# Cached latent attention: four sequences at once on the column quarters, all pages resident

## The chip, the cores and the metric

The kernel runs on one core of one Trainium2 chip. The metric is device time in microseconds (us). Every array is float32; matmuls of plain float32 operands appear in the trace as two records each, transposes as one.

## The reference

One decoder layer is computed for a prompt of 1024 positions and for 8 sample sequences of 4 new tokens each. Two token mixers run side by side: dilated window attention and multi-head latent attention. The change concerns the latent attention of the sample sequences, over 1024 cached positions that lie in pages of 128:

```python
ckv_past = cache_ckv[i][page_table].reshape(n_dec, past_len, B_KV_LORA)     # (8, 1024, 256)
kpe_past = cache_kpe[i][page_table].reshape(n_dec, past_len, B_ROPE_DIM)    # (8, 1024, 32)

def mla_sample(q_nope, q_pe, ckv_ext, kpe_ext, w_uk, w_uv):
    scale = (B_NOPE_DIM + B_ROPE_DIM) ** -0.5
    q_lat = jnp.einsum('nthe,che->nthc', q_nope, w_uk)
    s = (einsum('nthc,nkc->nhtk', q_lat, ckv_ext)
         + einsum('nthr,nkr->nhtk', q_pe, kpe_ext)) * scale
    p, _ = masked_softmax(s, jnp.arange(l)[None, :] <= qpos[:, None])
    o_lat = einsum('nhtk,nkc->nthc', p, ckv_ext)
    return einsum('nthc,che->nthe', o_lat, w_uv)
```

Each sequence has 8 heads x 4 tokens = 32 query rows, scored against 1028 keys (1024 cached, 4 new). A key has a latent part of 256 numbers, which serves as the value too, and a rotary part of 32.

## The kernel before

The program is a series of blocks with barriers between them: projections, the prompt's latent attention (`attend_latent`), the sample's latent attention (`attend_sample` with kind "latent"), the prompt's window attention, the sample's window attention (`attend_sample` with kind "window"), and a long tail (merge, output projection, MLP, embedding). Within a block each engine has its own list of instructions, in an order written out by hand, with semaphores between them.

`attend_sample` for the latent kind treats one sequence after another. A page number is read from an on-chip table into a register (line 1390) and the page is loaded (line 1391): the latent part by SyncE (SP), 128 KB a page, the rotary part by GpSimd (POOL). Keys live in a ring of four buffers `ls_keys`; the first is filled while `attend_latent` still runs (class `Ahead`, lines 1341 to 1375). For each of 8 tiles of 128 keys `turn_tile` transposes two latent halves (line 1522) and the rotary part (line 1524) into bank 3 or 4; ScalarE copies the even tiles and VectorE the odd ones to SBUF (lines 1445 to 1454, `take_keys`). `scores` multiplies the 32 query rows with the turned keys (1542 latent, 1544 rotary), into partitions 0 to 31. VectorE adds the mask and finds the maximum (1658), ScalarE takes the exponent (1461), VectorE divides (1665), TensorE transposes the probabilities (1553, 1554), VectorE copies them (1671, 1672). `values` multiplies them with the pages as loaded (1566) and with the new rows (1568); the result is copied (1709), transposed (1576) and copied again (1687). TensorE interleaves one tile's transposes for the sequence after next with one tile's value matmuls. After all sequences a projection with `w_uv` (1611) and four VectorE operations (1717, 1719) end the stage. In the middle of the stage SP also loads three of the four 1 MB pieces (`win_nat`) with which the next stage starts (1311).

`attend_latent` fills SP's list with the first pages and with eight copies of the cached window values from HBM to HBM (line 607), each waiting for a step of TensorE. Its scores and values (993, 1015) and the window stage's (1168, 1174, 1203, 1210) already use parts of the array: 1015 writes two column halves in turn, 1168 four column quarters with two row halves.

Lines that matter:

```python
            def scores(s):                      # 1525 on
                        for k in range(2):
                            pe.matmul(out, g.ql_t[:, k, s].rearrange("p h t -> p (h t)"), key_t[:, k, at:at + w],
                                      start=k == 0, stop=False)
```

Of the kernel before, what the change touches and what calls it, by code (L numbers as in the profile page):

```python
# [27 lines left out]
F32 = mybir.dt.float32  # L28
F32R = mybir.dt.float32r
I32 = mybir.dt.int32  # L30
ALU = mybir.AluOpType
# [3 lines left out]
P = 128  # L35
# [10 lines left out]
H = 8  # L46
# [10 lines left out]
SK = 5  # L57
EPS = 1e-6
# [85 lines left out]
def build(nc, io):  # L144

    with ExitStack() as ctx:
# [43 lines left out]
        g.w_uv_sb = room("w_uv_sb", [P, 2, H * E])  # L190
        g.ckv_t = room("ckv_t", [P, 2, T])
# [16 lines left out]
        g.latent_mask = Room(nc, Ahead.start_of("latent") - SEQ * BYTES)("latent_mask", [P, NT - 1, P])  # L208
# [737 lines left out]
def attend_latent(g, ahead):  # L946
# [151 lines left out]
RES = 4  # L1098
# [242 lines left out]
class Ahead:  # L1341
# [3 lines left out]
    @staticmethod  # L1345
    def start_of(kind):

        size = 2 * SK * H * E if kind == "window" else NPAGE * (KL + RD) + NSEQ * NPAGE
        return TOP // 32 * 32 - size * BYTES

    def __init__(self, g, kind):
        self.kind, self.start = kind, self.start_of(kind)
        room = Room(g.nc, self.start)
        if kind == "window":
            self.keys, self.vals = (room(f"ws_{n}0", [P, SK, H * E]) for n in ("keys", "vals"))
            self.k_in, self.v_in = ([g.sem(f"ws_{n}_in{j}") for j in range(3)] for n in "kv")
        else:
            self.keys = self.vals = room("ls_keys0", [P, NPAGE, KL + RD])
            self.pages = room("ls_pages", [1, NSEQ * NPAGE], I32)
            self.k_in, self.v_in = ([g.sem(f"ls_{n}_in{j}") for j in range(4)] for n in ("ckv", "kpe"))  # L1360
            self.pages_in = g.sem("pages_in")

    def load(self, g, sp):

        if self.kind == "window":
            load_cached_window(sp, g.cache_win_k, 0, self.keys, self.k_in[0])
            load_cached_window(sp, g.cache_win_v, 0, self.vals, self.v_in[0])
        else:
            sp.dma_start(self.pages[:, :], g.page_table.rearrange("(a s) n -> a (s n)", a=1)).then_inc(self.pages_in, 16)
            sp.wait_ge(self.pages_in, 16)  # L1370
            load_pages(sp, self.pages, 0, g.cache_ckv, self.keys[:, :, :KL], self.k_in[0])
# [15 lines left out]
def load_pages(eng, pages, s, cache, dst, arrived):  # L1387

    for n in range(NPAGE):
        page = eng.value_load(pages[0:1, s * NPAGE + n:s * NPAGE + n + 1], min_val=0, max_val=NPHYS - 1)  # L1390
        eng.dma_start(dst[:, n, :], cache[0, bass.ds(page, 1)].rearrange("a p c -> p (a c)")).then_inc(arrived, 16)  # L1391


def attend_sample(g, kind, ahead):
# [6 lines left out]
    window = kind == "window"  # L1401
    tag = "ws" if window else "ls"
    tiles = SK if window else NPAGE
    width = tiles * P + TDEC
    vcols = H * E if window else KL
    room = Room(nc, R2, RW if window else g.room_kept)
    sem = lambda name: g.sem(f"{tag}_{name}")
    if window:
        keys = [ahead.keys] + [room("ws_keys1", [P, SK, H * E])]
        vals = [ahead.vals] + [room(f"ws_vals{j}", [P, SK, H * E]) for j in (1, 2)]  # L1410
        unit_room(g, Room(nc, RW, RX), "tail")
        key_t = room("ws_key_t", [P, H // 2, width])
        q_new = room("ws_q_new", [NS, H * E])
        k_new = room("ws_k_new", [NS, H * E])
        k_new_t = room("ws_k_new_t", [P, H // 2, NS])
        q_rows = room("ws_q_rows", [P, H // 2, NSEQ, H, TDEC])
        v_new = room("ws_v_new", [TDEC, 3, H * E])
        v_new_in = [sem(f"v_new_in{j}") for j in range(3)]
    else:
        keys = [ahead.keys] + [room(f"ls_keys{j}", [P, NPAGE, KL + RD]) for j in (1, 2, 3)]  # L1420
        vals = keys
        key_t = room("ls_key_t", [P, 2, width])
        pe_t = room("ls_pe_t", [RD, width])
        v_new = room("ls_v_new", [TDEC, NSEQ, KL])
        o_t = room("ls_o_t", [P, 2, H, NSEQ, TDEC])
    mask = room(f"{tag}_mask", [NS, width])
    masked = room(f"{tag}_masked", [NS, width])
    prob = room(f"{tag}_prob", [NS, width])
    prob_t = room(f"{tag}_prob_t", [P, tiles + 1, NS])
# [13 lines left out]
    def take_keys(eng, s, odd):  # L1443
# [4 lines left out]
        for n in range(odd, tiles, 2):  # L1448
# [4 lines left out]
            if not window:  # L1453
                last = copy(pe_t[:, cols], g.bank[:RD, 3 + odd, 2 * P:3 * P])
# [746 lines left out]
```

## Time and profile before

| | us |
|---|---|
| median of 3 runs (2176.5 to 2183.6) | 2182.46 |
| the profiled execution | 2187.04 |
| its span | 2185.3 |

| engine | busy in the span | in the sample's latent stage (137.8 us) |
|---|---|---|
| TensorE matmul | 2077.8 us, 95% | 128.2 us |
| VectorE | 825.4 us, 38% | 47.1 us |
| ScalarE | 473.6 us, 22% | 26.2 us |
| GpSimd | 723.1 us, 33% | 30.7 us |

The span runs from the first to the last instruction; the execution's own time lies 1.7 us above it. The stage of the change runs from 714.6 to 852.4 us. The granted TensorE clock is given as a share of full speed: 1.00 is 2.4 GHz, 0.50 is 1.2 GHz.

### The profile page before, as it was taken

Reading aid. Unit: us, or ns where it says so; the run is one execution under the profiler, and the core shown is the slowest. Engines: PE = TensorE matmul, PEld = TensorE weight load, DVE = VectorE, ACT = ScalarE, POOL = GpSimd, SP = SyncE. Lnnn points to the kernel's source line nnn. Section 1 sums busy time; section 2 is a strip of 40 time slices with the busy share of each in tenths; the row PEclk is TensorE's granted clock in tenths of the full one; section 3 lists DMA queues with packets and bytes.
Section 4 is the critical chain, followed back from the end, with each engine's and each line's share of the span. In section 5 each row is a group of like instructions: output and inputs, shape, how many; then the busy total and the mean of one; then the engine's idle time right before and its main releaser. Section 6 shows DMA issues by size and latency. Waiting matters only on the chain. (4 is left out here: it accounts for less than half of the span.)

```text
span 2185.3 us, 34746 instructions
## 1 busy us (share of the span) xinstructions
PE 2077.8 (95%) x13121; PEld 1765.5 (81%) x13121; DVE 825.4 (38%) x1889; ACT 473.6 (22%) x1036; POOL 723.1 (33%) x483
## 2 busy tenths in 40 slices
PE   7899999999999898889989999999999999999898
PEld 7877799963566334663379999999999999999897
DVE  4245011153566334673334543212211211245565
ACT  4231111121455222551101211001100100112222
POOL 4223033300000320001036656535634644566431
PEclk9999999999999899999999999999999999999999
DMA  6333464400223443216354111111111111111212
GB/s 210 89 114 121 156 238 166 154 11 10 99 78 116 126 126 97 60 44 202 118 191 134 49 39 39 49 48 49 41 48 48 48 49 46 41 49 48 69 30 80
DMA packets 179831, 192.72 MB, mean 88 GB/s; under 512 B 11398, under 2 KB 152582, under 8 KB 178950
## 3 DMA queue, kind: packets, MB, share of 16 engines
q1 hardware_dynamic: 162854, 162.01, 23.4%
q10 hardware_dynamic: 14816, 28.12, 3.7%
q0 software_dynamic: 2048, 1.05, 0.2%
q8 instruction: 75, 1.23, 0.2%
q14 instruction: 38, 0.31, 0.0%
HBM read 160.74 MB, written 63.97 MB: 103 GB/s over the span
## 5 line engine op out<-in xcount | busy, mean ns | idle before, releaser
L635 PE MATMUL bank<-h_hi,wu_hi_tail 128*128 128x352 f32 x960 | 311.4, 324 | 3.4 <-POOL wu_lo_tail L1960 3.4
L636 PE MATMUL bank<-h_lo,wu_hi_tail 128*128 128x352 f32 x960 | 308.8, 322 | 0.0
L637 PE MATMUL bank<-h_hi,wu_lo_tail 128*128 128x352 f32 x960 | 308.7, 322 | 0.0
L1958 POOL TENSOR_TENSOR wu_hi_tail<-w_stage_tail,ones 128x1024 fp32r<-128x1024 f32 x88 | 169.9, 1931 | 407.1 <-DMA w_stage_tail<-in_w_ob 185.6
L635 PE MATMUL bank<-a_hi,wu_hi_tail 128*128 128x352 f32 x768 | 247.7, 323 | 0.0
L636 PE MATMUL bank<-a_lo,wu_hi_tail 128*128 128x352 f32 x768 | 246.1, 320 | 0.0
L637 PE MATMUL bank<-a_hi,wu_lo_tail 128*128 128x352 f32 x768 | 245.9, 320 | 0.0
L1960 POOL TENSOR_TENSOR wu_lo_tail<-w_stage_tail,wu_hi_tail 128x1024 fp32r<-128x1024 f32 x88 | 219.7, 2496 | 6.9
L635 PEld LDWEIGHTS bank<-h_hi,wu_hi_tail 128*128 128x128 f32 x960 | 180.9, 188 | 3.7 <-issue 3.7
L636 PEld LDWEIGHTS bank<-h_lo,wu_hi_tail 128*128 128x128 f32 x960 | 181.2, 189 | 0.0
L637 PEld LDWEIGHTS bank<-h_hi,wu_lo_tail 128*128 128x128 f32 x960 | 181.0, 189 | 0.0
L1915 ACT ACTIVATE a_hi<-f_hg 128x352 f32 x96 | 48.0, 500 | 602.8 <-DVE f_hg L2021 602.8
L2004 DVE TENSOR_TENSOR x_res<-bank,x_res 128x352 f32 x120 | 62.9, 525 | 300.6 <-PE bank L637 300.4
L1391 POOL DMA_DIRECT2D ls_keys<-in_cache_kpe x64 | 35.6, 556 | 349.1 <-issue 349.1
L636 PEld LDWEIGHTS bank<-a_lo,wu_hi_tail 128*128 128x128 f32 x768 | 144.3, 188 | 0.0
L635 PEld LDWEIGHTS bank<-a_hi,wu_hi_tail 128*128 128x128 f32 x768 | 144.1, 188 | 0.0
L637 PEld LDWEIGHTS bank<-a_hi,wu_lo_tail 128*128 128x128 f32 x768 | 143.9, 187 | 0.0
L1970 POOL TENSOR_TENSOR a_lo<-f_hg,a_hi 128x352 f32 (+1 forms) x96 | 91.2, 950 | 144.9 <-ACT a_hi L1915 144.9
L2018 DVE TENSOR_TENSOR f_tmp<-bank,rstd_bc 128x352 f32<-128x352 f32 x96 | 50.3, 524 | 234.6 <-PE bank L637 234.4
L432 PE MATMUL bank<-wn_hi,h_hi 128*128 128x512 f32 (+5 forms) x360 | 133.7, 371 | 0.0
L434 PE MATMUL bank<-wn_hi,h_lo 128*128 128x512 f32 (+5 forms) x360 | 131.7, 366 | 0.0
L433 PE MATMUL bank<-wn_lo,h_hi 128*128 128x512 f32 (+5 forms) x360 | 131.2, 364 | 0.0
(288 smaller groups left out, 3968.5 us busy)
## 6 DMA issues: line engine op xcount, KB each, us to landing
w_stage_tail<-in_w_up SPq DMA_DIRECT2D x32, 512.0 KB, 4.0
w_stage_tail<-in_w_down SPq DMA_DIRECT2D x32, 512.0 KB, 3.6
gate_d<-gate_out ACTq DMA_DIRECT2D x16, 528.0 KB, 2.9
f_gates<-gate_d ACTq DMA_DIRECT2D x24, 352.0 KB, 3.1
w_stage_gates<-in_w_in SPq DMA_DIRECT2D x16, 512.0 KB, 3.8
ls_keys<-in_cache_ckv SPq DMA_DIRECT2D x64, 128.0 KB, 2.1
ws_keys<-in_cache_win_k SPq DMA_DIRECT2D x8, 1024.0 KB, 7.2
ws_vals<-in_cache_win_v SPq DMA_DIRECT2D x8, 1024.0 KB, 6.5
```

Of the source, the lines that this page charges most:

```text
L432: pe.matmul(out, a, w, start=k == 0, stop=False)
L433: pe.matmul(out, a, v, start=False, stop=False)
L434: last = pe.matmul(out, c, w, start=False, stop=k == KD - 1)
L635: pe.matmul(out, w, a, start=n == 0, stop=False)
L636: pe.matmul(out, w, b, start=False, stop=False)
L637: last = pe.matmul(out, v, a, start=False, stop=n == len(ks) - 1)
L1915: act.activation(chunk_of(st.out[0], i, q), g.hg[:, q % 2:q % 2 + 1, :], ACT.Copy).then_inc(g.hi_s, 1)
L1958: pool.tensor_tensor(g.wu_hi[:, j], g.w_stage[:, j], one, ALU.mult).then_inc(g.w_hi, 1)
L1960: pool.tensor_tensor(g.wu_lo[:, j], g.w_stage[:, j], g.wu_hi[:, j].bitcast(F32), ALU.subtract).then_inc(g.w_split, 1)
L1970: pool.tensor_tensor(chunk_of(st.out[1], i, q), g.hg[:, q % 2:q % 2 + 1, :], chunk_of(st.out[0], i, q).bitcast(F32), ALU.subtract).then_in ...
L2004: dve.tensor_tensor(x, g.bank[:, q:q + 1, :CH], x, ALU.add).then_inc(g.free, 1)
L2018: dve.tensor_tensor(g.tmp[:, q % 2, :], g.bank[:, q, :CH], g.rstd_bc[:, c * CH:(c + 1) * CH], ALU.mult).then_inc(g.free, 1)
```

## The change

The class `Ahead` is split into `CachedPages` and `CachedWindow`, and `attend_sample` into `attend_latent_sample` and `attend_window_sample`; the window part is the same as before. In the latent part:

- Each sequence's pages have a buffer of their own. Three sequences are loaded while `attend_latent` runs (`early = 3`), into places free at that time; the other five at the stage's start, into the places of the prompt's queries, keys and values. Their 40 page numbers are read into registers ahead (`find_rest`), during `attend_latent`.
- All rotary pages are loaded by GpSimd during `attend_latent`, as 32 lines of 4 rows x 32 numbers each instead of 128 lines of 32, four pages one under another.
- Sequences are treated in two batches of four. Sequence s of a batch writes its 32 rows of scores and values to partitions 32s to 32s+31. Mask, exponent and transposes then work on 128 partitions, once per batch.
- Transposes go in groups: two tiles x two halves in one bank and one copy of 512 columns; the rotary keys of a sequence are two transposes. The rotary scores take four matmuls of 128 columns, one for each residue j of the key's position, against queries padded with zeros (`q_pad`), written to every fourth column.
- The new keys are scored by matmuls of their own (4 columns) rather than copied beside the turned keys. The division by the sum moves from the probabilities to the result (32 x 1028 per sequence before, 128 x 256 per batch after).
- SP's order at the stage's start is: 40 pages, four loads of `q_pad`, four of the mask, the new rows, then the three `win_nat` loads for the next stage.

```diff
-        for kind in ("latent", "window"):
-            ahead = Ahead(g, kind)
-            (attend_window if kind == "window" else attend_latent)(g, ahead)
-            attend_sample(g, kind, ahead)
+        pages = CachedPages(g)
+        attend_latent(g, pages)
+        attend_latent_sample(g, pages)
+        cached = CachedWindow(g)
+        attend_window(g, cached)
+        attend_window_sample(g, cached)
...
             for s in range(NSEQ):
                 sp.wait_ge(o_got, s * (N // NSEQ) + 1)
                 copy_cache(sp, g, g.cache_win_v, g.win_v_sample, s, 1)
+                if s == NSEQ // 2:
+                    ahead.find_rest(sp)
...
+class CachedPages:
+    start = TOP // 32 * 32 - (NPAGE * KL + NSEQ * NPAGE) * BYTES
+    early = 3
+    def __init__(self, g):
+        nc = g.nc
+        room = Room(nc, self.start)
+        first_keys = room("ls_keys0", [P, NPAGE, KL])
+        self.pages = room("ls_pages", [1, NSEQ * NPAGE], I32)
+        low = Room(nc, R1 + KD * T * BYTES, R1 + (KD + H // 2) * T * BYTES)
+        kept = Room(nc, R2, g.room_kept)
+        self.key_t = kept("ls_key_t", [P, BATCH, 2, PAST])
+        self.rope_t = kept("ls_rope_t", [P, BATCH, 2, P])
+        self.keys = [first_keys] + [low(f"ls_keys{s}", [P, NPAGE, KL]) for s in range(1, self.early)]
+        self.keys += [kept(f"ls_keys{s}", [P, NPAGE, KL]) for s in range(self.early, NSEQ)]
+        self.v_new = kept("ls_v_new", [TDEC, BATCH, KL])
+        self.rope = []
+        for b in range(2):
+            at = g.ckv_t_at + b * T * BYTES
+            self.rope.append(Room(nc, at, at + SEQ * BYTES)(f"ls_rope{b}", [P, BATCH, 2, RES * RD]))
+        self.pages_in, self.rope_in = g.sem("pages_in"), g.sem("rope_in")
+        self.k_in = [g.sem(f"ls_k_in{s}") for s in range(NSEQ)]
+    def page(self, eng, s, n):
+        at = s * NPAGE + n
+        return eng.value_load(self.pages[0:1, at:at + 1], min_val=0, max_val=NPHYS - 1)
+    def load_keys(self, g, sp, s, page_of):
+        for n in range(NPAGE):
+            src = g.cache_ckv[0, bass.ds(page_of(n), 1)].rearrange("a p c -> p (a c)")
+            sp.dma_start(self.keys[s][:, n, :], src).then_inc(self.k_in[s], 16)
+    def load(self, g, sp):
+        sp.dma_start(self.pages[:, :], g.page_table.rearrange("(a s) n -> a (s n)", a=1)).then_inc(self.pages_in, 16)
+        sp.wait_ge(self.pages_in, 16)
+        for s in range(self.early):
+            self.load_keys(g, sp, s, lambda n: self.page(sp, s, n))
+    def find_rest(self, sp):
+        self.found = {(s, n): self.page(sp, s, n) for s in range(self.early, NSEQ) for n in range(NPAGE)}
+    def load_rest(self, g, sp):
+        for s in range(self.early, NSEQ):
+            self.load_keys(g, sp, s, lambda n: self.found[s, n])
     def load_rotary(self, g, pool):
         pool.wait_ge(self.pages_in, 16)
-        load_pages(pool, self.pages, 0, g.cache_kpe, self.keys[:, :, KL:], self.v_in[0])
+        for s in range(NSEQ):
+            for n in range(NPAGE):
+                lo = RD * (n % 4)
+                src = g.cache_kpe[0, bass.ds(self.page(pool, s, n), 1)].rearrange("a (k j) r -> (a k) (j r)", j=RES)
+                pool.dma_start(self.rope[s // BATCH][lo:lo + RD, s % BATCH, n // 4, :], src).then_inc(self.rope_in, 16)
...
+def attend_latent_sample(g, ahead):
...
+    def take_keys(copy, eng, s, odd):
+        if s >= BATCH:
+            eng.wait_ge(s_full, s // BATCH)
+        for q in range(groups):
+            n = s * groups + q
+            if n % 2 != odd:
+                continue
+            eng.wait_ge(k_full, n + 1)
+            src = g.bank[:, 3 + odd, :]
+            if q < groups - 1:
+                copy(key_t[:, s % BATCH, :, 2 * q * P:2 * (q + 1) * P], src.rearrange("p (k c) -> p k c", k=2)).then_inc(k_got[odd], 1)
+            else:
+                copy(rope_t[:, s % BATCH, :, :].rearrange("p a c -> p (a c)"), src[:, :2 * P]).then_inc(k_got[odd], 1)
+    with nc.Block() as block:
+        @block.sync
+        def _(sp):
+            ahead.load_rest(g, sp)
+            sp.wait_ge(pad_set, 1)
+            for j in range(RES):
+                sp.dma_start(q_pad[RD * j:RD * (j + 1), j, :, :], g.qpe_t[:, :, :, :].rearrange("r s h t -> r s (h t)")).then_inc(pad_in, 16)
+            for j in range(BATCH):
+                sp.dma_start(mask[rows(j), :], g.mask_ls_c).then_inc(mask_in, 16)
+            v_src = g.ckv_sample[0].rearrange("s t c -> t s c")
+            sp.dma_start(v_new[:, :, :], v_src[:, :BATCH, :]).then_inc(v_new_in, 16)
+            load_queries_and_keys(g, sp, (0, 1, 2))
+            sp.wait_ge(o_full, 1)
+            sp.dma_start(v_new[:, :, :], v_src[:, BATCH:, :]).then_inc(v_new_in, 16)
+        @block.gpsimd
+        def _(pool):
+            pool.memset(q_pad[:, :, :, :].rearrange("p j s c -> p (j s c)"), 0.0).then_inc(pad_set, 1)
+        @block.tensor
+        def _(pe):
+            def turn_keys(s):
+                for q in range(groups):
+                    n = s * groups + q
+                    if q == 0:
+                        pe.wait_ge(ahead.k_in[s], 16 * NPAGE)
+                    if n == groups - 1:
+                        pe.wait_ge(ahead.rope_in, 16 * NSEQ * NPAGE)
+                    if n >= 2:
+                        pe.wait_ge(k_got[n % 2], n // 2)
+                    if q < groups - 1:
+                        for k in range(2):
+                            for a in range(2):
+                                at = (2 * k + a) * P
+                                last = pe.transpose(g.bank[:, 3 + n % 2, at:at + P], keys[s][:, 2 * q + a, k * P:(k + 1) * P], g.ident[:, :])
+                    else:
+                        for a in range(2):
+                            last = pe.transpose(g.bank[:, 3 + n % 2, a * P:(a + 1) * P], rope[s // BATCH][:, s % BATCH, a, :], g.ident[:, :])
+                    last.then_inc(k_full, 1)
+            def scores(b):
+                done = groups * BATCH * (b + 1) // 2
+                for odd in range(2):
+                    pe.wait_ge(k_got[odd], done)
+                if b == 0:
+                    pe.wait_ge(pad_in, 16 * RES)
+                else:
+                    pe.wait_ge(s_got, b)
+                    pe.wait_ge(pt_high, b)
+                latent = lambda k, s: g.ql_t[:, k, s].rearrange("p h t -> p (h t)")
+                for c in range(2):
+                    for k in range(2):
+                        for s in batch(b):
+                            pe.matmul(g.bank[rows(s), c, :], latent(k, s), key_t[:, s % BATCH, k, c * 512:(c + 1) * 512],
+                                      start=k == 0, stop=False)
+                    for j in range(RES):
+                        for s in batch(b):
+                            out = g.bank[rows(s), c, :].rearrange("p (n m j) -> p n m j", n=4, j=RES)[:, :, :, j]
+                            pe.matmul(out, q_pad[:, j, s, :], rope_t[:, s % BATCH, c, :].rearrange("p (n m) -> p n m", n=4),
+                                      start=False, stop=j == RES - 1)
+                for k in range(2):
+                    for s in batch(b):
+                        new = slice(SEQ + s * TDEC, SEQ + (s + 1) * TDEC)
+                        pe.matmul(g.bank[rows(s), 2, :TDEC], latent(k, s), g.ckv_t[:, k, new], start=k == 0, stop=False)
+                for s in batch(b):
+                    last = pe.matmul(g.bank[rows(s), 2, :TDEC], g.qpe_t[:, s].rearrange("p h t -> p (h t)"),
+                                     g.kpe_t[:, s * TDEC:(s + 1) * TDEC], start=False, stop=True)
+                last.then_inc(s_full, 1)
+            def turn_probs(b):
+                pe.wait_ge(e_done, b + 1)
+                if b >= 1:
+                    pe.wait_ge(pt_low, b)
+                    pe.wait_ge(pt_high, b)
+                for n in range(NPAGE):
+                    last = pe.transpose(g.bank[:, 5 + n // 4, n % 4 * P:(n % 4 + 1) * P], prob[:, n * P:(n + 1) * P], g.ident[:, :])
+                    if n == 3:
+                        last.then_inc(pt_full, 1)
+                pe.transpose(g.bank[:TDEC, 2, P:2 * P], prob[:, PAST:], g.ident[:, :]).then_inc(pt_full, 1)
+            def values(b):
+                pe.wait_ge(pt_low, b + 1)
+                pe.wait_ge(pt_high, b + 1)
+                pe.wait_ge(v_new_in, 16 * (b + 1))
+                if b >= 1:
+                    pe.wait_ge(ot_got, b)
+                for n in range(NPAGE):
+                    for s in batch(b):
+                        pe.matmul(g.bank[rows(s), 7, :KL], prob_t[:, n, rows(s)], keys[s][:, n, :], start=n == 0, stop=False)
+                for s in batch(b):
+                    last = pe.matmul(g.bank[rows(s), 7, :KL], prob_t[:TDEC, NPAGE, rows(s)], v_new[:, s % BATCH, :], start=False, stop=True)
+                last.then_inc(o_full, 1)
+            def turn_result(b):
+                pe.wait_ge(o_taken, b + 1)
+                for k in range(2):
+                    last = pe.transpose(g.bank[:, 7, KL + k * P:KL + (k + 1) * P], o_nat[:, k * P:(k + 1) * P], g.ident[:, :])
+                last.then_inc(ot_full, 1)
+            for s in batch(0):
+                turn_keys(s)
+            scores(0)
+            turn_keys(4)
+            turn_keys(5)
+            turn_probs(0)
+            turn_keys(6)
+            values(0)
+            turn_keys(7)
+            turn_result(0)
+            scores(1)
+            turn_probs(1)
+            values(1)
+            turn_result(1)
+            pe.wait_ge(ot_got, 2)
...
+        @block.scalar
+        def _(act):
+            copy = lambda out, src: act.activation(out, src, ACT.Copy)
+            def exponent(b):
+                act.wait_ge(s_got, b + 1)
+                act.activation(prob[:, :], prob[:, :], ACT.Exp, scale=-1.0, bias=top[:, b, 0:1],
+                               accum_out=top[:, b, 2:3]).then_inc(e_done, 1)
...
+        @block.vector
+        def _(dve):
+            def largest(b):
+                dve.wait_ge(s_full, b + 1)
+                if b >= 1:
+                    dve.wait_ge(pt_full, 2 * b)
+                dve.tensor_tensor_reduce(out=prob[:, :], in0=g.bank[:, 0:3, :].rearrange("p a b -> p (a b)")[:, :PAST + TDEC],
+                                         in1=mask[:, :], scale=-1.0, scalar=-FLOOR, op0=ALU.add, op1=ALU.min,
+                                         accum_out=top[:, b, 0:1]).then_inc(s_got, 1)
...
+            for s in batch(0):
+                take_keys(dve.tensor_copy, dve, s, 1)
+            dve.wait_ge(mask_in, 16 * BATCH)
+            largest(0)
+            take_keys(dve.tensor_copy, dve, 4, 1)
+            take_keys(dve.tensor_copy, dve, 5, 1)
+            invert(0)
+            take_probs(0)
+            take_keys(dve.tensor_copy, dve, 6, 1)
+            take_values(0)
+            take_keys(dve.tensor_copy, dve, 7, 1)
+            take_result(0)
+            largest(1)
+            invert(1)
+            take_probs(1)
+            take_values(1)
+            take_result(1)
...
```

## Rows read from the trace of the kernel before

**Rows 1.** TensorE's timeline at the stage's start: start us, us, line, count [idle before].
```profile
712.31 0.97 PE L1015 MATMUL bank<-latent_prob_t,vb 128*64 128x128 f32 x12
714.64 0.41 PE L1522 MATMUL bank<-ident,ls_keys 128*128 128x128 f32 x2 [1.35 <-PEq L970]
```

**Rows 2.** Stretches: length, busy us of each engine, PEclk, DMA share, GB/s.
```profile
714.64:852.40 137.76, 128.22 (x600) 47.41 (x600) 47.10 (x149) 26.24 (x80) 30.73 (x56) 0.95 0.31 93
745.00:762.00 17.00, 16.83 (x82) 6.23 (x81) 5.87 (x19) 3.27 (x10) 3.11 (x6) 1.00 0.13 38
728.00:731.00 3.00, 1.38 (x10) 0.95 (x11) 1.04 (x4) 1.81 (x6) 1.27 (x3) 1.00 0.49 142
732.00:745.00 13.00, 11.45 (x26) 2.81 (x25) 2.25 (x8) 0.53 (x2) 5.53 (x10) 0.51 0.45 125
```

**Rows 3.** TensorE's timeline: scores at half and full clock, values in a row.
```profile
735.86 3.62 PE L1542 MATMUL bank<-ls_key_t,ql_t 128*32 128x512 f32 x4
...
755.64 1.90 PE L1542 MATMUL bank<-ls_key_t,ql_t 128*32 128x512 f32 x4
...
761.62 0.44 PE L1522 MATMUL bank<-ident,ls_keys 128*128 128x128 f32 x2
...
838.96 3.64 PE L1566 MATMUL bank<-ls_keys,ls_prob_t 128*32 128x256 f32 x16
```

**Rows 4.** Groups by shape, 712 to 853 us: count, busy us, mean ns.
```profile
L1566 PE MATMUL bank<-ls_keys,ls_prob_t 128*32 128x256 f32 x128 | 35.9, 387 | 0.4 <-DVE ls_prob_t L1672 0.4
L1542 PE MATMUL bank<-ls_key_t,ql_t 128*32 128x512 f32 x64 | 33.9, 656 | 0.9 <-DVE ls_pe_t L1637 0.9
L1522 PE MATMUL bank<-ident,ls_keys 128*128 128x128 f32 x128 | 27.5, 302 | 4.6 <-ACT ls_pe_t L1445 2.4 <-PEq L970 1.4 <-DMA ls_keys<-in_cache_ckv 0.6
L1524 PE MATMUL bank<-ident,ls_keys 128*32 128x128 f32 x64 | 17.9, 279 | 0.0
L1544 PE MATMUL bank<-ls_pe_t,qpe_t 32*32 32x512 f32 x32 | 17.5, 628 | 0.0
```

**Rows 5.** TensorE's timeline in the window stage: eight parts of the array, then the next group.
```profile
867.45 0.56 PE L1168 MATMUL bank<-kw_c,qw_c 64*32 64x192 f32 x16 [0.88 <-DVE kw_c L1338]
867.94 0.60 PE L1174 MATMUL bank<-kw_c,qw_c 64*128 64x128 f32 x6
```

**Rows 6.** SP: timeline of the page loads, median of the pieces, sizes and landing.
```profile
578.06 133.40 SPq L607 DMA_DIRECT2D out_win_v_sample<-in_cache_win_v  x8
716.18 13.24 SPq L1391 DMA_DIRECT2D ls_keys<-in_cache_ckv  x12
L1391 SPq DMA_DIRECT2D ls_keys<-in_cache_ckv x64: 332/333/881, 558.1 to 809.5; - x64
1038.33 1.70 SPq L1383 DMA_DIRECT2D ws_keys<-in_cache_win_k  x4
ls_keys<-in_cache_ckv SPq DMA_DIRECT2D x64, 128.0 KB, 2.1
```

**Rows 7.** Timeline of the window's sample stage: groups of four transposes through two banks.
```profile
988.41 1.09 PE L1522 MATMUL bank<-ident,ws_keys 128*128 128x128 f32 x8 [1.44 <-ACT ws_key_t L1445]
989.10 0.60 ACT L1445 ACTIVATE ws_key_t<-bank 128x512 f32<-128x512 f32 x1 [0.74 <-PE bank L1522]
989.53 0.69 DVE L1452 COPY ws_key_t<-bank 128x512 f32<-128x512 f32 x1 [1.77 <-PE bank L1522]
989.75 0.66 PE L1522 MATMUL bank<-ident,ws_keys 128*128 128x128 f32 x4 [0.25 <-ACT ws_key_t L1445]
```

**Rows 8.** A stretch in which 1 MB loads fill the DMA engines (columns as in rows 2).
```profile
764.00:770.00 6.00, 6.00 (x30) 2.37 (x29) 2.43 (x8) 2.29 (x7) 0.45 (x1) 1.00 0.89 278
```

**Rows 9.** Groups of the other engines, and the projection's timeline.
```profile
L1658 DVE CUSTOM_DVE_ANT_0 ls_masked<-bank,ls_mask 32x1028 f32<-32x1028 f32 x8 | 9.7, 1217 | 48.9 <-PE bank L1544 48.9
L1461 ACT ACTIVATE ls_prob<-ls_masked,ls_top 32x1028 f32<-32x1028 f32 x8 | 9.1, 1141 | 17.5 <-DVE ls_top L1658 17.5
849.70 1.15 PE L1611 MATMUL bank<-ls_o_t,w_uv_sb 128*64 128x32 f32 x32 [0.32 <-DVE ls_o_t L1687]
```

More of the change, by code:

```diff
@@ L1384, in load_cached_window @@
     sp.dma_start(dst[:, 1:, :], cache[0, s, PAST // 2:].rearrange("(a p) h e -> p a (h e)", p=P)).then_inc(arrived, 16)
[L1387 to L1394, printed above, removed]
-    nc = g.nc
-    window = kind == "window"
-    tag = "ws" if window else "ls"
-    tiles = SK if window else NPAGE
-    width = tiles * P + TDEC
[L1405 to L1429, printed above, removed]
-    top = room(f"{tag}_top", [NS, 2, 4])
-    o_nat = room(f"{tag}_o_nat", [NS, vcols])
@@ new lines, in attend_window_sample @@
+def attend_window_sample(g, ahead):
+    nc = g.nc
+    tiles = SK
+    width = tiles * P + TDEC
+    vcols = H * E
+    room = Room(nc, R2, RW)
+    sem = lambda name: g.sem(f"ws_{name}")
+    keys = [ahead.keys] + [room("ws_keys1", [P, SK, H * E])]
+    vals = [ahead.vals] + [room(f"ws_vals{j}", [P, SK, H * E]) for j in (1, 2)]
+    unit_room(g, Room(nc, RW, RX), "tail")
+    key_t = room("ws_key_t", [P, H // 2, width])
+    q_new = room("ws_q_new", [NS, H * E])
+    k_new = room("ws_k_new", [NS, H * E])
+    k_new_t = room("ws_k_new_t", [P, H // 2, NS])
+    q_rows = room("ws_q_rows", [P, H // 2, NSEQ, H, TDEC])
+    v_new = room("ws_v_new", [TDEC, 3, H * E])
+    v_new_in = [sem(f"v_new_in{j}") for j in range(3)]
+    mask = room("ws_mask", [NS, width])
+    masked = room("ws_masked", [NS, width])
+    prob = room("ws_prob", [NS, width])
+    prob_t = room("ws_prob_t", [P, tiles + 1, NS])
+    top = room("ws_top", [NS, 2, 4])
+    o_nat = room("ws_o_nat", [NS, vcols])
@@ L1450, in take_keys @@
             cols = slice(n * P, (n + 1) * P)
[L1451 to L1455 removed]
+            copy(key_t[:, :, cols], g.bank[:, 3 + odd, :].rearrange("p (k c) -> p k c", k=4)).then_inc(k_got[odd], 1)
     def exponent(act, s):
@@ L1495, in _ @@
         @block.gpsimd
         def _(pool):
[L1497 to L1507 removed]
+            for j in range(2):
+                pool.wait_ge(g.w_loaded[j], (g.turns + 2) * 16)
+                split_weights(pool, g, j, g.units + j + 1)
@@ L1520, in turn_tile @@
                 b = 3 + n % 2
-                for k in range(4 if window else 2):
+                for k in range(4):
                     last = pe.transpose(g.bank[:, b, k * P:(k + 1) * P], keys[s % k_ring][:, n, k * P:(k + 1) * P], g.ident[:, :])
-                if not window:
-                    last = pe.transpose(g.bank[:RD, b, 2 * P:3 * P], keys[s % k_ring][:, n, KL:], g.ident[:, :])
                 last.then_inc(k_full, 1)
@@ L1567, in values @@
                 else:
-                    pe.matmul(g.bank[:NS, 6, :vcols], prob_t[:TDEC, tiles, :], v_new[:, s % v_ring if window else s, :],
+                    pe.matmul(g.bank[:NS, 6, :vcols], prob_t[:TDEC, tiles, :], v_new[:, s % v_ring, :],
                               start=False, stop=True).then_inc(o_full, 1)
@@ L1604, in _ @@
             turn_result(NSEQ - 1)
-            if not window:
-                pe.wait_ge(ot_got, NSEQ)
-                for h in range(H):
-                    lo = E * (h % 2)
-                    for c in range(2):
-                        last = pe.matmul(g.bank[lo:lo + E, 5 + h % 2, (h // 2) * NS:(h // 2 + 1) * NS], g.w_uv_sb[:, c, h * E:(h + 1) * E],
-                                         o_t[:, c, h].rearrange("p s t -> p (s t)"), start=c == 0, stop=c == 1)
-                last.then_inc(ot_full, 1)
         @block.scalar
```

250 lines of the change are left out of this document (125 added, 125 removed).

## The prediction

> **What bounds the kernel now.** I read the page's shares first, then the busy times of single stretches, then the shapes and the timeline inside the stage that the change rewrites. TensorE is busy in nearly all of the span, in every stage, so a stage is worth what its TensorE work and its waits take, and stages follow each other behind barriers: what one saves, the end saves. The rewritten stage, latent attention over the cached pages, runs from the first transpose of cached keys at 714.64 to the first instruction of the window stage at 852.4: 137.8 us [rows 1, 2]. In it TensorE is busy 128.2 us, and is fully busy in the middle (16.83 of 17 us), while VectorE has 47 us, ScalarE 26 us and the DMA engines 31% [rows 2]. So it is bound by TensorE's own stream, not by data. One sequence costs 15.5 us at full clock (scores 755.64 to 761.62). 13 us of the stage ran at half clock [rows 2, 3].
>
> **What goes.** The old matmuls use 32 of 128 columns: 32 query rows per sequence, always in the first column quarter. By shape they are 64 latent score records of 512 columns, 33.9 us; 32 rotary ones, 17.5 us; 128 value records, 35.9 us; and 192 transposes, 45.4 us [rows 4].
>
> **Do quarters run at once?** The trace of before has no four-quarter matmul over all 128 rows, so I bound it. Four 512-column records in one quarter take 1.90 us with the last one's latency of 0.6, 0.43 to 0.46 apart [rows 3]. Sixteen records of 192 columns on 64 rows by 32 columns (two row halves, four column quarters) start at 867.45 and the next group starts at 867.94: 0.49 us. One after another, at that rate (about 0.16 us for 192), they would take 2.6 us. Twelve records of 128 columns over all 128 rows, alternating between the two column halves, take 0.97 us with the last one's latency of some 0.27, about 0.06 us each, where eight 128-column transposes take 1.09 us, 0.11 each [rows 1, 5, 7]. Halves over 128 rows share fully, quarters over 64 rows share nearly fully. I take four at once; the other end is none at once.
>
> The Trainium skill, "TensorE: Matmul & The Clock Gate", Part 3, gives 2.38 times for three column tiles with 512 columns, some 80% of perfect. By that figure, as an estimate, the streams below would be about 5 us longer. The trace's 0.49 us against 2.6 us already contains such losses.
>
> **What the new stage costs on TensorE, at full clock.**
> - Scores of one batch of four: 32 records of 512 columns are 8 rounds of four, 8 x 0.43 = 3.4 us. 64 rotary records of 128 columns (four residues against a zero-padded query, written with a stride) are 16 x 0.11 = 1.8 us. 24 records of four columns are 0.3 us. With latency 5.6 us, where four sequences took 4 x 6.0 [rows 3].
> - Values of one batch: 72 records of 256 columns, 18 rounds. The old 16 in a row took 3.64 us, 0.217 each [rows 3], so 18 x 0.217 + 0.2 = 4.1 us.
> - Turning keys: per sequence 18 transposes instead of 24 (rotary keys come four rows to a 128-wide line), but in five groups of up to four that go through two banks. The window's sample stage has this very loop: groups start at 988.41 and 989.75 on one bank, the ScalarE copy takes 0.60 and the VectorE copy 0.69, the latter ending at 990.22 [rows 7]. So a pair of groups needs 1.44 us, a group 0.72, a sequence 3.6. Copies bound it, not the transposes.
>
> The strided write of the rotary scores has no row. Nearest are contiguous writes of the same size; below, it costs nothing; above, a rate halved adds 1.8 us per batch. I take nothing.
>
> **When data is there.** Three sequences' pages come during the prompt's latent stage. SP there issues 24 page DMAs instead of 8, at 1.10 us each with its read 18 us more, and reads 40 page numbers between two cache copies, at most 27 us; the queue only waits there to issue 8 copies over 133 us [rows 6]. The last copy waits for its step, at 711, as before. GpSimd issues 64 rotary DMAs there, and was idle. Both cost nothing; if that cover were gone, the loads at the stage's start would come up to 45 us later.
>
> At the stage's start SP issues the other 40 pages. A page took 1.10 us, of which the DMA instruction is 0.33; the rest is reading its number and preparing the address. Without the read a bare load has 0.43 (four in 1.70), and half of the 1.10 would be 0.55 [rows 6]. I take 0.5, address steps included: 20 us. 5.2 MB at the 278 GB/s seen with win_nat loads is 19 us, the same [rows 8]. Behind these, in SP's order, stand the four small DMAs that fill the padded queries and four for the mask, and TensorE's first scores wait for the queries. So scores can start at 714.4 + 20 + 1.7 + 2.1 (landing) = 738.5; the ends are 735 and 741. Four sequences are turned by 714.6 + 14.4 = 729, or 3 later if the fourth's pages hold it. **The new wait is some 9 us of idle TensorE for the padded queries**, and everything after stands behind it.
>
> **From there, at full clock:** scores 5.6; VectorE's mask and maximum 1.3 and ScalarE's exponent 1.35, both ahead of their key copies (1.22 and 1.14 on 32 partitions, taken as the same on 128) [rows 9]; two sequences turned 7.2; probabilities turned 1.1; third sequence 3.6 with 0.9 of probability copies; values 4.1; fourth sequence 3.6; result and last key copy 1.2: 30.0 us. Second batch: 5.6 + 2.65 + 1.1 + 0.9 + 4.1 + 1.1 for the result, 1.15 for the value projection, 1.2 for its four copies and 0.5 to the next stage: 18.3 us [rows 9]. The next stage then starts at 738.5 + 48.3 = 786.8 instead of 852.4: 65.6 us saved.
>
> **The clock.** In before, a stretch where TensorE transposed through two banks and waited (1.38 of 3 us busy at 728 to 731) was followed by 13 us at half clock, from 731 to 745, through 9 us of continuous score matmuls; scores then took 3.62 us where they take 1.90 [rows 2, 3]. The new stage has this kind of stretch for longer, then the idle wait. If everything after 738 ran at half clock, scores add 11.2, values 8.2, transposes and the rest 3, and each of 20 groups 0.2: 26.6 us. I take a third, 9 us: the first scores and part of what follows.
>
> The Trainium skill, same page, Part 4, says transposes do not count as busy for the clock. By that rule the turning stretches would keep the clock low all through; that gives the second case below. The trace is mixed: full clock in the old middle with transposes between value matmuls.
>
> **Sum.** 65.6 - 9 = 56.6 us. The profiled execution took 2187.04 us around a span of 2185.3 and goes to 2130.4; it lies 4.6 above the median of the runs, 2182.46, which goes to **2126 us**.
>
> **Rivals.**
> - Half clock throughout: 2182.5 - 65.6 + 26.6 = 2143.5 us. For it: [rows 2]. Against: dense value and score blocks between.
> - Everything kinder: queries there at 735 and no clock loss: 2182.5 - 69 = 2113.5 us.
> - Quarters take turns, so that the change doesn't do what it says: scores become 32 x 0.43 + 64 x 0.11 + 1.2 = 22 us, values 15.6, which adds 16.4 and 11.5 per batch, 56 us: no change, 2182 us. Against: the 0.49 us of [rows 5].
> - The other side: each change of quarter drains the array, so that every record pays its latency instead of its pitch: 32 x 0.66 + 64 x 0.28 = 39 us of scores (the transposes' 0.28 for 128 columns) and 72 x 0.39 = 28 us of values [rows 4], 57 us more per batch than forecast, 115 us in all: 2126 + 115 = 2241 us. It decides from 28 us more per batch. Against it: the alternating halves of line 1015 [rows 1], 12 records in 0.97 us, where each alone would pay 0.28.
>
> **Chances.** Forecast 0.70, half clock 0.12, kinder 0.12, turns 0.04, drain 0.02. The 80% range is 2109 to 2149: the kinder case less 4 for cheaper issues, and the half-clock case plus 5 for slower pages and the strided writes. Faster by over 0.3% (6.5 us, about what a measurement here can tell): 0.95; same 0.03; slower 0.02.
>
> **What would show it.** Scores of four sequences in about 5.6 us, records of four quarters starting within some 10 ns of each other; values in about 4; TensorE idle before the first scores until the padded queries land, near 738; groups of transposes 0.72 us apart; the window stage starting near 796 with the 9 us of clock loss. It is wrong if the 512-column records of the quarters start 0.4 us apart, if key pages arrive later than 0.5 us each, or if the prompt's latent stage (before 714) gets longer through the added DMAs.

## The result and the profile after

| | before | after |
|---|---|---|
| median of the runs shown | 2181.5 us (4 runs) | 2123.9 us (4 runs, 2122.4 to 2125.6) |
| ratio, with 95% interval | | 0.9727 [0.9707, 0.9746] |
| span of the profiled execution | 2185.3 us | 2121.4 us |

The forecast was 2126 us; 57.6 us were saved where 56.6 were foreseen. Between the two profiled executions the difference is 63.9 us (2187.04 and 2123.12): the one before lies 4.6 us above the median of its runs, the one after 0.8 us below. The timelines give the lengths of the stages from the first instruction of each (the last two borders from SP's first load); "half" is the time that the records show at half clock:

| us | before | half | after | half |
|---|---|---|---|---|
| up to the sample's latent stage | 714.6 | | 713.9 | |
| sample's latent stage | 137.8 | 13.7 | 77.3 | 23.9 |
| window stage | 120.1 | 17.1 | 117.6 | 17.9 |
| window's sample stage | 129.9 | 17.1 | 128.8 | 19.6 |
| tail | 1082.9 | 24.0 | 1083.9 | 25.7 |

So 60.5 of the span's 63.9 us are from the rewritten stage. TensorE's timeline in it, after (answers to [rows 1, 3, 7]):

```profile
713.85 1.06 PE L1511 MATMUL bank<-ident,ls_keys 128*128 128x128 f32 x8 [1.21 <-PEq L975]
...
724.17 1.10 PE L1511 MATMUL bank<-ident,ls_keys 128*128 128x128 f32 x8 [0.57 <-DMA ls_keys<-in_cache_ckv]
725.62 1.09 PE L1511 MATMUL bank<-ident,ls_keys 128*128 128x128 f32 x8 [0.35 <-DVE ls_key_t L1471]
...
739.98 3.64 PE L1530 MATMUL bank<-ls_key_t,ql_t 128*32 128x512 f32 x16 [12.48 <-DMA ls_q_pad<-qpe_t]
743.36 1.40 PE L1535 MATMUL bank<-ls_rope_t,ls_q_pad 128*32 128x128 f32 x32
744.57 1.91 PE L1530 MATMUL bank<-ls_key_t,ql_t 128*32 128x512 f32 x16
746.28 1.06 PE L1535 MATMUL bank<-ls_rope_t,ls_q_pad 128*32 128x128 f32 x32
...
750.84 1.97 PE L1511 MATMUL bank<-ident,ls_keys 128*128 128x128 f32 x8 [2.21 <-ACT ls_key_t L1600]
...
761.20 3.66 PE L1565 MATMUL bank<-ls_keys,ls_prob_t 128*32 128x256 f32 x64
...
769.31 1.92 PE L1530 MATMUL bank<-ls_key_t,ql_t 128*32 128x512 f32 x16 [0.34 <-issue]
...
774.72 0.24 PE L1542 MATMUL bank<-kpe_t,qpe_t 32*32 32x4 f32 x8
777.60 1.49 PE L1552 MATMUL bank<-ident,ls_prob 128*128 128x128 f32 x8 [2.64 <-ACT ls_prob L1604]
...
780.32 5.94 PE L1565 MATMUL bank<-ls_keys,ls_prob_t 128*32 128x256 f32 x64 [1.02 <-issue]
...
791.12 2.37 PE L1328 MATMUL bank<-ident,win_nat 128*128 128x128 f32 x20 [1.58 <-PEq L1475]
```

Sixteen 512-column records, four per quarter, take 1.91 us, where in [rows 3] four in one quarter took 1.90. The second batch's scores run from 769.31 to 774.96, 5.7 us. The idle time of 12.48 us before the first scores ends with the padded queries. SP's timeline in the prompt's latent stage and at the stage's start (answers to [rows 6]):

```profile
557.49 26.40 SPq L1397 DMA_DIRECT2D ls_keys<-in_cache_ckv  x24
583.94 126.88 SPq L612 DMA_DIRECT2D out_win_v_sample<-in_cache_win_v  x8
713.95 22.06 SPq L1397 DMA_DIRECT2D ls_keys<-in_cache_ckv  x40
736.06 2.48 SPq L1482 DMA_DIRECT2D ls_q_pad<-qpe_t  x4
```

Forty pages in 22.06 us are 0.55 us each, and the small loads stand behind all of them. The stage as a whole and pieces of it (columns as in [rows 2]):

```profile
714.60:791.00 76.40, 49.95 (x577) 31.75 (x575) 20.02 (x38) 14.57 (x26) 0.16 (x1) 0.84 0.41 133
728.00:740.00 12.00, 0.03 (x4) 0.06 (x5) 0.00 (x0) 0.00 (x0) 0.00 (x0) 0.60 0.71 212
...
757.00:765.40 8.40, 7.94 (x102) 5.13 (x102) 2.76 (x6) 2.35 (x5) 0.00 (x0) 1.00 0.01 2
...
780.00:787.00 7.00, 6.50 (x72) 3.17 (x72) 0.33 (x3) 0.00 (x0) 0.00 (x0) 0.64 0.01 2
```

TensorE is busy 50 of 76 us where it was 128 of 138. By shape, 714 to 795 us (answers to [rows 4]):

```profile
L1511 PE MATMUL bank<-ident,ls_keys 128*128 128x128 f32 x128 | 19.0, 292 | 6.8 <-ACT ls_key_t L1600 2.8 <-DVE ls_key_t L1471 2.1 <-PEq L975 1.2
L1565 PE MATMUL bank<-ls_keys,ls_prob_t 128*32 128x256 f32 x128 | 9.6, 465 | 1.0 <-issue 1.0
L1530 PE MATMUL bank<-ls_key_t,ql_t 128*32 128x512 f32 x64 | 9.4, 710 | 12.8 <-DMA ls_q_pad<-qpe_t 12.5 <-issue 0.3
L1535 PE MATMUL bank<-ls_rope_t,ls_q_pad 128*32 128x128 f32 x128 | 4.6, 285 | 0.0
```

The same 128 value records take 9.6 us instead of 35.9, the same 64 latent score records 9.4 instead of 33.9.

### The profile page after: what moved, and what is told of

It is laid out like the page before. It is cut to its first block, busy times and chain, and to the rows that moved or that the text cites. A ratio compares the mean times of both kernels' runs of the same rounds, so it can differ in the third digit from the quotient of the medians.

```text
span 2121.4 us, 34495 instructions
## 1 busy us (share of the span) xinstructions
PE 2001.8 (94%) x13103; PEld 1752.9 (83%) x13103; DVE 796.7 (38%) x1778; ACT 460.9 (22%) x982; POOL 721.2 (34%) x484
## 4 chain that ended last, share of the span: by engine, by line
PE 46%; DVE 1%; DMA 1%; issue 1%; POOL 1%; ACT 1%; DVEq 0%; ACTq 0%; POOLq 0%
PE bank L640 15%; PE bank L641 15%; PE bank L642 15%; DMA f_gates<-gate_d 1%; DVE x_res L2254 0%; PE bank L2321 0%; PE bank L2282 0%; DVE f_diag L2339 0%; PE bank L2284 0%; PE bank L2283 0%; PE bank L2358 0%; DMA out_y_prompt<-y_nat 0%; PE bank L2311 0%; POOL wu_lo_tail L2177 0%; DVE f_hg L2252 0%
## 5 line engine op out<-in xcount | busy, mean ns | idle before, releaser
L640 PE MATMUL bank<-h_hi,wu_hi_gates 128*128 128x352 f32 x384 | 124.7, 325 | 3.7 <-PEq L311 3.7
```

Source lines behind the costliest of these rows:

```text
L640: pe.matmul(out, w, a, start=n == 0, stop=False)
```

## The experiments

All are edits of the changed kernel. Ratios are to the kernel before, runs on the same chip; "stage" is the sample's latent stage in the profiled execution (77.3 us in the changed kernel). The experiments ran in three series on three chips, where the kernel before had medians of 2183.6, 2182.2 and 2183.8 us against 2181.5 beside the changed kernel. So a difference of medians between rows can be some 2 us off; the ratios are free of this, and where the two differ the text gives both.

| run | median us | ratio, 95% interval | stage us |
|---|---|---|---|
| changed kernel | 2123.9 | 0.9727 [0.9707, 0.9746] | 77.3 |
| turns | 2164.9 | 0.9910 [0.9889, 0.9931] | 116.5 |
| turns_values | 2140.6 | 0.9802 [0.9781, 0.9824] | 93.2 |
| read_late | 2150.0 | 0.9835 [0.9814, 0.9855] | 101.7 |
| pad_pool | 2114.4 | 0.9676 [0.9658, 0.9694] | 67.0 |
| warm | 2122.2 | 0.9748 [0.9723, 0.9773] | 75.0 |
| banks4 | 2123.7 | 0.9724 [0.9708, 0.9739] | 74.3 |
| pad_mid | 2114.5 | 0.9695 [0.9671, 0.9720] | 63.4 |
| mid_banks4 | 2110.4 | 0.9668 [0.9653, 0.9682] | 61.2 |
| mid_v | 2105.5 | 0.9641 [0.9627, 0.9654] | 60.3 |
| mid_v_busy | 2102.9 | 0.9623 [0.9604, 0.9642] | 57.5 |

**turns and turns_values: one quarter after another.**

```diff
-                    for k in range(2):
-                        for s in batch(b):
-                            pe.matmul(g.bank[rows(s), c, :], latent(k, s), ...)
+                    for s in batch(b):
+                        for k in range(2):
+                            pe.matmul(g.bank[rows(s), c, :], latent(k, s), ...)
...
-                for n in range(NPAGE):
-                    for s in batch(b):
+                for s in batch(b):
+                    for n in range(NPAGE):
                         pe.matmul(g.bank[rows(s), 7, :KL], prob_t[:, n, rows(s)], keys[s][:, n, :], ...)
```

The rotary scores' loop is turned in the same way in turns.

> The changed kernel with the loop over the four sequences moved outside the loops over key halves, residues and tiles, in scores and in values: the same matmuls, but successive ones stand on the same column quarter. Theory (the gain is that four quarters stream at once): scores become 32 x 0.43 + 64 x 0.11 + 0.4 = 21 us and values 15.6 us a batch, where the changed kernel shows 5.6 (full clock) and 4.2: 27 us more a batch, 54 in all, so about 2124 + 54 = 2178 us, near the kernel before. Rival (the gain is mostly the resident pages, fewer transposes and fewer steps per sequence, and TensorE reorders what it can): under 15 us more, 2124 to 2139 us.

> As the kernel with both loops turned, but only the loop of the values is turned. Theory: values take 15.6 us a batch instead of 3.7 at full clock, 11.5 to 12 us more each, 2124 + 23 = 2147 us. Rival (TensorE pulls matmuls of other quarters ahead, so the order does not matter): 2124 us.

Measured: 41 us more for both loops (54 expected), 17 more for the values alone (23 expected); by the ratios 40 and 16. So the theory holds in kind and is about a quarter too high, and one rival has a part of the truth. The values of the first batch, turns_values, timeline:

```profile
763.33 11.50 PE L1565 MATMUL bank<-ls_keys,ls_prob_t 128*32 128x256 f32 x64
774.76 0.63 PE L1567 MATMUL bank<-ls_v_new,ls_prob_t 4*32 4x256 f32 x8
```

11.50 us against 3.66 is 7.8 more, not 12. One after another at 0.216 us, 64 would take 13.8. The single records' starts show why: inside a quarter they are 216 ns apart, but at each of the three borders the last four of a quarter and the first four of the next start in pairs 6 to 30 ns apart. TensorE overlaps a few records across a border, though not sixteen. In turns, the second batch's scores take 18.3 us instead of 5.7, with overlap at the borders too: the last four rotary records of one quarter run beside the first latent record of the next. The two blocks of scores and the two of values there are longer by 12.8, 12.7, 7.8 and 7.2 us, 40.5 together, and the stage by 39.2: the loss lies in these blocks.

What follows: the order that lets four quarters run at once is worth 41 us of the 57.6; against a program without any overlap it would be more, since a part is left at the borders. The remaining 17 us are what the rest of the change brings, its new waits included; no run takes these apart.

**read_late: reading the page numbers at the stage's start.**

```diff
-            self.load_keys(g, sp, s, lambda n: self.found[s, n])
+            self.load_keys(g, sp, s, lambda n: self.page(sp, s, n))
```

and without the call of `find_rest`.

> The changed kernel without the reading ahead of page numbers: each of the 40 pages at the stage's start has its number read just before its load, 1.10 us a page instead of 0.55. Theory (TensorE's idle time before the first scores hangs on SP's issue of the 40 pages, ahead of the padded queries): the first scores start 22 us later, and since nothing else of the stage can move before them, 2124 + 22 = 2146 us. Rival (the DMA engines' rate set the arrival, not the issue): clearly less, under 10 us.

Timelines of read_late, SP and TensorE:

```profile
715.60 43.60 SPq L1395 DMA_DIRECT2D ls_keys<-in_cache_ckv  x40
763.14 3.64 PE L1528 MATMUL bank<-ls_key_t,ql_t 128*32 128x512 f32 x16 [34.51 <-DMA ls_q_pad<-qpe_t]
```

Measured: 26 us more (runs from 2145 to 2160), 24 by the ratios. SP issues the 40 pages in 43.60 us instead of 22.06. The first scores start 48.3 us after the stage's start instead of 26.1, the expected 22 us. The stage is 24.4 us longer; the idle time of 34.5 us is followed by more half clock, 54 us in the stage. SP's issue sets the time, and the rival falls.

**pad_pool and pad_mid: the small loads earlier.**

```diff
 pad_pool, GpSimd's list:
             pool.memset(q_pad..., 0.0).then_inc(pad_set, 1)
+            pool.wait_ge(pad_set, 1)
+            (the four q_pad loads and the four mask loads, on pool)
 pad_mid, in load_rest:
         for s in range(self.early, NSEQ):
             self.load_keys(g, sp, s, lambda n: self.found[s, n])
+            if s == self.early:
+                small()      # the same eight loads, on sp
```

In both, these eight loads are gone from their old place behind the 40 pages.

> The changed kernel with the four loads of padded queries and the four of the mask issued by GpSimd, right after its fill with zeros, instead of by SP behind the 40 pages. Theory: the first scores no longer wait for them but for the fourth sequence's turned keys, at about 728 instead of 740, and all after moves with it: 12 us less, 2112 us; the first scores then run at full clock, perhaps 1 to 2 us less again. Rival (the fifth to eighth sequence's pages, of which the last lands near 738, are the next bound, or the clock takes it back): under 5 us less.

> The changed kernel with the four loads of padded queries and the four of the mask issued by SP right behind the fourth sequence's eight pages, ahead of the other 32. Theory: the first scores wait for the fourth sequence's turned keys (pages landed near 724, turned by 727.5), 12 us earlier than now; the later pages come 4.5 us later than now (last near 742) and are needed later still (sequence 5 from 733, 8 from 752): 2124 - 12 = 2112 us, or 2 less since the scores run at full clock, so 1 to 4 us better than with GpSimd as issuer (2114.4). Rival (the later pages are the next bound): 2114 to 2118 us.

Measured: 9.5 us less with each by the medians, 11 and 7 by the ratios; the two intervals overlap. In pad_pool the first scores start 17.6 us after the stage's start instead of 26.1, and the stage is 10.3 us shorter. TensorE waits 3.2 us for the fourth sequence's pages, and goes on with them 2.7 us later than in the changed kernel. GpSimd's loads are under way then, but that they are the cause is not shown. In pad_mid, timeline:

```profile
727.38 0.44 PE L1518 MATMUL bank<-ident,ls_rope 128*128 128x128 f32 x2 [0.35 <-DVE ls_key_t L1473]
728.38 1.92 PE L1534 MATMUL bank<-ls_key_t,ql_t 128*32 128x512 f32 x16 [0.56 <-issue]
```

The wait is gone, the scores start 14.0 us after the stage's start and run at full clock, and the stage is 13.9 us shorter, as the theory has it. The whole gained only 9.5 in the median (runs from 2108.7 to 2121.2); the profiled run of 2111.2 gained 12. By the stage the later pages hold nothing back; by the whole I can't tell a gain over pad_pool.

**warm: extra transposes in the idle time.**

```diff
                 if b == 0:
+                    for x in range(96):
+                        pe.transpose(g.bank[:, x // 4 % 3, x % 4 * P:(x % 4 + 1) * P], g.ident[:, :], g.ident[:, :])
                     pe.wait_ge(pad_in, 16 * RES)
```

> The changed kernel with 96 extra transposes of the identity (into banks 0 to 2, overwritten afterwards) between the fourth sequence's turned keys and the wait for the padded queries, 10.5 us of work inside an idle time of 12.5 us. Theory (the idle time is what puts the first scores on half clock): the first score matmuls take 1.9 us for 16 instead of 3.6, and 2 to 3 us are saved, 2121 to 2122 us. Rival 1 (transposes do not keep the clock up): the scores still take 3.6 us and the time stays at 2124 us. Rival 2 (the clock loss moves to a later stretch): scores at full clock, but the time stays.

Timeline of warm:

```profile
726.07 10.67 PE L1523 MATMUL bank<-ident 128*128 128x128 f32 x96 [0.61 <-DVE ls_rope_t L1473]
738.47 1.92 PE L1532 MATMUL bank<-ls_key_t,ql_t 128*32 128x512 f32 x16 [1.73 <-DMA ls_q_pad<-qpe_t]
```

The scores take 1.92 us instead of 3.64 and the stage is 2.3 us shorter: the idle time had put the first scores on half clock, and back-to-back transposes do hold the clock, which was granted in full from 712 to 749 us. In the whole no gain is shown (2118 to 2135; by the ratios, whose intervals overlap, warm is 0.2% slower). The two slowest runs, 2131.3 and 2134.7, have a mean granted clock of 0.972 and 0.969, the other three 0.976 to 0.978, and no trace, so rival 2 stays open for them.

**banks4: four banks for the transposes.**

```diff
+    bank_of = lambda n: 3 + n % (4 if n < 30 else 2)
...
-            src = g.bank[:, 3 + odd, :]
+            src = g.bank[:, bank_of(n), :]
...
-                    if n >= 2:
-                        pe.wait_ge(k_got[n % 2], n // 2)
+                    if n >= (4 if n < 30 else 2):
+                        pe.wait_ge(k_got[n % 2], n // 2 - (1 if n < 30 else 0))
```

The first probabilities' transposes get a wait for the copies out of banks 5 and 6.

> The changed kernel with the groups of transposes of the first six sequences going through banks 3 to 6 instead of 3 and 4 (the transposes of the first probabilities then wait for the copies out of banks 5 and 6). Theory (turning is bound by the copy's round trip through two banks, 0.72 us a group): groups come 0.45 to 0.65 us apart; in the first four sequences nothing is gained, since TensorE waits for the padded queries anyway; the fifth and sixth take 5 us instead of 7.2: 2 us less, 2122 us. Rival (turning is bound by TensorE or by the half clock): no change.

Timeline of banks4:

```profile
714.38 1.94 PE L1512 MATMUL bank<-ident,ls_keys 128*128 128x128 f32 x16 [1.21 <-PEq L975]
716.15 0.38 PE L1515 MATMUL bank<-ident,ls_rope 128*128 128x128 f32 x2
716.37 1.91 PE L1512 MATMUL bank<-ident,ls_keys 128*128 128x128 f32 x16
...
723.96 3.55 PE L1512 MATMUL bank<-ident,ls_keys 128*128 128x128 f32 x16 [3.49 <-DMA ls_keys<-in_cache_ckv]
```

A sequence is turned in 2.0 us instead of 3.4 to 3.6: two banks were the bound. The first four gain nothing, since the pages and then the queries are waited for. The stage is 3.0 us shorter, the whole the same: the window stage of that profiled run was 2.3 us longer (119.9 against 117.6, with 24.3 us at half clock against 17.9).

**mid_banks4, mid_v, mid_v_busy: put together.** mid_v also loads the new value rows with the small loads; mid_v_busy adds:

```diff
             scores(1)
+            keep_busy(22)     # transposes of the identity into bank 3
             turn_probs(1)
+            keep_busy(8)
             values(1)
```

> Both the loads of padded queries and mask behind the fourth sequence's pages, and four banks for the transposes of the first six sequences. Theory: on top of the first change, the fourth sequence is turned in 2.4 us instead of 3.4 after its pages land, and the fifth and sixth in 5 instead of 7.2 us, as far as their pages are there (5.5 us apart): 2 to 3 us better than the moved loads alone, near 2109 us. Rival (the pages of sequences 5 and 6 now hold TensorE back): no better than the moved loads alone.

> The kernel with the moved small loads and four banks, and with the load of the new value rows moved ahead too, behind the mask. Theory (that kernel had 1.2 us of TensorE waiting for these rows before the first values): this wait goes, the stage takes 60 us instead of 61.2, the whole 2109 us. Rival: the fifth sequence's pages, 0.5 us later, take it back; 2110 us.

> As the kernel before it, with 22 transposes of the identity between the second batch's scores and its probabilities (a wait of 2.6 us) and 8 more before its values (a wait of 1.0 us), into a bank that nobody reads. Theory (these waits put the second batch's values on half clock, where 64 matmuls take 5 to 6.5 us instead of 3.7): the values take 3.7 us, the stage 58 instead of 60 us, the whole 2 to 3 us less, 2106 to 2107 us. Rival 1: the extra transposes overrun the waits or do not hold the clock, no change. Rival 2: the half clock moves into the window stage, the stage of the change gets shorter and the whole stays.

Each shortened the stage: 61.2, 60.3, 57.5 us. mid_banks4 ran into a wait of 1.2 us for the new value rows, which mid_v took away; mid_v's whole came out lower than expected, 2105.5, and by more than the 1.0 us of the stage, which stays unexplained (the intervals just overlap). Timeline of mid_v_busy:

```profile
759.12 2.63 PE L1580 MATMUL bank<-ident 128*128 128x128 f32 x22
761.83 1.10 PE L1560 MATMUL bank<-ident,ls_prob 128*128 128x128 f32 x8
762.76 0.27 PE L1563 MATMUL bank<-ident,ls_prob 128*4 128x128 f32 x1
762.87 1.04 PE L1580 MATMUL bank<-ident 128*128 128x128 f32 x8
764.05 3.66 PE L1573 MATMUL bank<-ls_keys,ls_prob_t 128*32 128x256 f32 x64
```

The extra work fits the waits, and the values take 3.66 us instead of 6.43 in mid_v. Its whole, 2102.9 us, is 21 us below the changed kernel and its interval lies clear of it. Its interval overlaps mid_v's, so the busy work is shown in the stage and not in the whole. In the profiled runs the half clock did not move into the window stage, as rival 2 has it: that took 119.4 us with 23.7 at half clock, in mid_v 122.2 with 30.1.

## Why the prediction was right, point by point

- **Bound by TensorE's stream.** Right: TensorE's busy time in the stage fell by 77.5 us and the stage by 60.5; the rest turned into waits.
- **Four quarters at once.** Right, and without loss. The gap from the first 16 records to what follows is 1.71 us, 0.107 a record, where one quarter alone needs 0.43: 4.0 times. The Trainium skill ("TensorE: Matmul & The Clock Gate", Part 3) has 2.38 times for three column tiles; the measurement decides, and here four tiles lose nothing. By turns, it is worth 41 us. The drain rival falls: starts in different quarters are 6 to 7 ns apart.
- **Scores 5.6 us, values 4.1 us.** Measured 5.7 and 4.2 at full clock. The strided write costs nothing visible: 32 records of 128 columns take 1.06 us, 0.87 to the next, 0.027 each, a quarter of the 0.11 of plain transposes.
- **Turning, 0.72 us a group.** Measured 0.72 (724.17 to 725.62 for two), and banks4 shows its cause.
- **0.5 us a page.** Too small: 0.55, so 2 us later. The four small loads took 2.48 us to issue, where the 1.7 in the sum was taken from plain loads. TensorE went on 1.4 us after the last of them was issued, where 2.1 was taken for the landing. The first scores started 26.0 us after SP's first page, forecast 24.1 (the sum 714.4 + 20 + 1.7 + 2.1 itself gives 738.2, not 738.5). That is one of three terms that were mis-sized, by 2 us.
- **The new wait.** Right in place, cause and consequence (read_late, pad_pool, pad_mid), 12.5 us instead of 9.
- **The stretch behind the first scores.** Forecast 48.3 us at full clock. The shortest that each of its pieces took in the changed kernel, warm and pad_mid, with 3.66 us for both batches' values, adds up to 46.1 us, so it was some 2 us too high. The error lies between the first scores and the first values: 15.5 us were added up, 13.6 measured in the changed kernel, since the mask, maximum and exponent made TensorE wait 2.2 us, not their whole 2.65, and the copies of the probabilities, 0.9 us in the sum, ran beside its transposes.
- **The clock.** Right in kind (warm), about double in size: 9 us were forecast. From the first scores to the next stage it took 51.1 us where 48.3 plus 9 was forecast; above the 46.1 it is 5.0. The first scores lost 2.0 us, the second batch's values 2.3, the rest lies in between. The records show 23.9 us at half clock in the stage, but TensorE was idle in 9.6 of them, 730.4 to 740.0. (The case of half clock throughout adds up to 26.4 us, not 26.6.)
- **The total.** The late start cost 2 us; the two terms behind it came out 6 us lower. So the window stage started at 791.1 where near 796 was forecast, and the stage saved 60.5 us in the trace, 3.9 more than the sum. That the medians moved by 57.6, 1 us from the 56.6, is luck in part: the late start hid a third of the error behind it, and the profiled executions came out 63.9 us apart, of which 5.4 are how far each lies from its median.
- **The covers.** Right: the prompt's latent stage did not get longer (713.9 against 714.6), and the eight copies kept their place with 26.40 us of page loads ahead.
- **Not foreseen:** some 3 us outside the stage, in the two window stages, whose code is unchanged. In the profiled runs of the changed kernel and its variants the window stage takes 117.6 to 117.9 us with 17 to 18 us at half clock, 119.3 to 119.9 with 21 to 27, 122.2 to 122.5 with 30, and 129.1 with 47. So how much half clock falls there moves the whole by some us, and this can hide small gains of a stage. The executions without a trace fit: in pad_mid, 2108.7 and 2111.2 us (the traced one) go with a mean granted clock of 0.976, 2117.9 and 2121.2 with 0.970 and 0.968. The kernel before (120.1 us with 17.1) doesn't lie on this line; what set it apart stays open.

## What to carry to other kernels

Where a matmul's result has 32 rows, give four independent ones a column quarter each and put them next to each other in the order of instructions; the same matmuls quarter after quarter give back most of the gain. Once a stage is short, look at what stands in front of its first matmul in a queue: eight small loads behind forty large ones cost 10 to 14 us of the stage here. Judge small changes by the stage in the trace as well as by the whole, since half clock in later stages can hide some us (117.6 to 122.5 us for the same window stage, read_late left out).

## What the hardware showed that was not expected

- TensorE overlaps records across a border of quarters: four on each side of it started in pairs 6 to 30 ns apart, while inside a quarter they were 216 ns apart.
- Back-to-back transposes hold the clock: after 96 of them in 10.67 us the scores ran at full clock. The Trainium skill ("TensorE: Matmul & The Clock Gate", Part 4) says that transposes do not count as busy; here the measurement differs.
- After 2.6 and 1.0 us of waiting with nine transposes between, 64 value records took 5.0 to 6.5 us in eight of the profiled runs and 3.66 us where the waits were filled.
